# Copies of cached keys and values moved from the MLP to the projection, issued tile by tile

## The chip, the cores and the metric

The kernel runs on one core of one Trainium2 chip. The metric is the device time of one execution in microseconds, from the runs of the kernel on the chip; a profile of one execution gives the trace. SyncE (SP) only issues DMA transfers and waits on semaphores; ScalarE (ACT) computes and issues transfers too. TensorE is PE, VectorE is DVE, GpSimd is POOL.

## What is computed

One layer of a hybrid decoder for a prompt of 2048 rows and a sample group of 8 sequences with 8 rows each, all in float32. The part of the reference that the change touches is the new window of the sample group: the cached keys and values without their first 8 rows, and the 8 new rows behind them.

```python
D_MODEL, BATCH, SEQ, DEC_BATCH, DEC_SEQ = 1024, 1, 2048, 8, 8     # WB = 2048 cached rows, 8 heads of 64
def layer(hp, hs):
    a = mixer(rms_norm(h, norm1_g))        # proj = h @ w_in; dilated attention || mLSTM; @ w_out
    h = h + a
    h = h + square(relu(rms_norm(h, norm2_g) @ w_up)) @ w_down       # D_FF = 4096
# in the mixer of the sample group:
kc = concatenate([win_k, ka], axis=1)      # win_k: (8, 2048, 8, 64), ka: the 8 new rows
vc = concatenate([win_v, va], axis=1)
new_k, new_v = kc[:, -2048:], vc[:, -2048:]
```

Outputs are the final normalised rows, the new windows, and the mLSTM states.

## The kernel before

The program runs in stages: `project` (the input projection), `mixers` (attention and mLSTM), `project_out`, and `mlp`. Products are made in three parts of rounded numbers (high x high, low x high, high x low; `split_products`, L220 to L222), so each weight is rounded by ACT and its rest taken by POOL or DVE before PE can use it.

**The projection.** Rows are taken in two groups, of 8 and of 9 tiles of 128 rows. Per group PE makes 8 chunks of conv columns and then five token blocks b = 0 to 4 (`tokens`, q, k, v, output gate and mLSTM value), each of 512 columns for every tile of the group. A tile's products go to one of two banks in turn and add 1 to `tok_mm`; PE starts tile t+2 when DVE has emptied tile t (`tok_ready`). DVE empties a bank into a slot of `stage` (`tile_out`, L659 to L663); the first group uses two slots in turn, the second three, and DVE waits until the slot's last store has landed (`stage_out`). ACT issues that store (`keep`, L501) right after DVE. In the second group the last tile holds the sample's rows and is the eighth of nine in order; it needs two thirds of the products.

The weights of a block are loaded by SP into one buffer, `w_raw` (L368 in the first group, L372 in the second), as soon as the block before has been split from it (`lo_ready`). ACT rounds a block (`round_block`, L463) one block ahead of its use, between the stores of two blocks, and POOL takes the rests (L411). In the second group SP's queue also carries, in this order, the tables of the mLSTM gates: `sync_load` and `sync_ends` behind the load of block 2, `sync_m` (two round trips of the running maximum through DRAM), eight staged tiles (`load_tile`, L346) and `sync_weights` behind the load of block 3, then `sync_sample` and the other staged tiles behind the load of block 4. ACT reads the gate rows after the third tile of block 1 (`act_log`), DVE the maximum after the third tile of block 2.

```python
with sp.Fori(1, 5) as b:                                     # first group
    sp.wait_ge(lo_ready, b + (base + 8))
    sp.dma_start(w_raw[:], K.w_tok[b]).then_inc(wt_in, 16)
```

**The MLP.** Three groups of 6, 6 and 5 tiles; per group 16 steps f of 256 hidden columns. SP loads `wu_raw` (L2649) and `wd_raw` (L2652) when POOL is done with the buffer, and ahead of that each step issues two copies, `copy` (L2683): step f = 2i + j of group g copies the part 2g + j, of six, of the cached keys and of the values of sequence i. A copy is 340 rows of 2 KB, contiguous, from DRAM to DRAM; 3 groups x 16 steps x 2 make 96 copies. The steps 0 to 11 are a loop on SP, 12 to 15 are written out. The second and third group begin with loads of tiles of x (`load_x`, L2657) and of the residual (L2673). Nothing reads the copies; SP waits for all of them at the end of the program.

Of the kernel before, what the change touches and what calls it, by code (L numbers as in the profile page):

```python
# [16 lines left out]
DEC_B, DEC_T = 8, 8  # L17
# [10 lines left out]
WB = 2048  # L28
# [213 lines left out]
def project(K):  # L242

    nc, sem = K.nc, K.sem
# [5 lines left out]
    with ExitStack() as ctx:  # L251
# [77 lines left out]
        def _(sp):  # L329
# [11 lines left out]
            def load_tile(x):  # L341
# [3 lines left out]
                    rows = rows.rearrange("(e u) c -> u e c", u=16)  # L345
                sp.dma_start(staged[:, x], rows).then_inc(staged_in, 16)  # L346

            for g in range(2):
                if g == 0:
                    norm.sync_group(sp, GN[0], constants)  # L350
                else:
                    for T in range(GT0[1], GT0[1] + GN[1]):
                        norm.load(sp, T, T % 2, False)
                        if T == GT0[1] + 1:
                            sp.wait_ge(lo_ready, 13)
                            load_first()
                base = 13 * g
                sp.wait_ge(norm.xn_ready, 8 + 8 * g)
                sp.dma_start(wq_raw, K.w_qk[1]).then_inc(wq_in, 16)
                sp.wait_ge(qk_mm, QB[g] + NPC[g])  # L360
                sp.dma_start(w_raw[:], K.w_tok[0]).then_inc(wt_in, 16)
                with sp.Fori(2, 8) as c:
                    sp.wait_ge(lo_ready, c + base)
                    sp.dma_start(wq_raw, K.w_qk[c]).then_inc(wq_in, 16)
                if g == 0:
                    with sp.Fori(1, 5) as b:
                        sp.wait_ge(lo_ready, b + (base + 8))
                        sp.dma_start(w_raw[:], K.w_tok[b]).then_inc(wt_in, 16)  # L368
                    continue
                for b in range(1, 5):  # L370
                    sp.wait_ge(lo_ready, b + (base + 8))
                    sp.dma_start(w_raw[:], K.w_tok[b]).then_inc(wt_in, 16)  # L372
                    if b == 2:
                        for s in range(2):
                            sp.wait_ge(acc_out[s], 16 * 8)
                        sp.wait_ge(conv_out, 16)
                        tables.sync_load(sp)
                        tables.sync_ends(sp)
                    if b == 3:
                        tables.sync_m(sp)  # L380
                        for s in range(3):
                            sp.wait_ge(stage_out[s], 16 * (6 + (20 if s < 2 else 0)))
                        for x in range(24, 32):
                            load_tile(x)
                        tables.sync_weights(sp)
# [2206 lines left out]
def mlp(K):  # L2592
# [7 lines left out]
    FB = DFF // 256  # L2600
    G = len(GN)
    with ExitStack() as ctx:
# [20 lines left out]
        assert nc.sbuf_base <= K.front_at + 4 * TOP  # L2623
        bank = K.bank

        acc_in, y_out, copied = sem("mlp_acc_in"), sem("mlp_y_out"), sem("mlp_copied")
        wu_in, wu_hi_ready, wu_lo_ready = M.wu_in, M.wu_hi_ready, M.wu_lo_ready
        wd_in, wd_hi_ready, wd_lo_ready = sem("mlp_wd_in"), sem("mlp_wd_hi"), sem("mlp_wd_lo")
        up_mm, u2_ready, u_hi_ready, u_lo_ready = sem("mlp_up_mm"), sem("mlp_u2"), sem("mlp_u_hi"), sem("mlp_u_lo")
# [13 lines left out]
        block = ctx.enter_context(nc.Block(no_gpsimd_drain=True))  # L2643
        @block.sync
        def _(sp):
            CB = (WB - DEC_T) // 6

            def load_up(E, f):
                sp.dma_start(wu_raw[:], K.ins["w_up"][f]).then_inc(wu_in, 16)  # L2649

# [8 lines left out]
            for g in range(G):  # L2659
# [18 lines left out]
                    sp.wait_ge(wd_lo_ready, 1)  # L2678
                    load_down(1, 1)

                def copy(i, j):
                    for name in ("k", "v"):
                        sp.dma_start(K.o[f"win_{name}_sample"][0].rearrange("b s h d -> b s (h d)")[i, CB * (2 * g + j):CB * (2 * g + j + 1), :],  # L2683
                                     K.ins["cache_" + name][i, DEC_T + CB * (2 * g + j):DEC_T + CB * (2 * g + j + 1), :])\
                            .then_inc(copied, 16)

                def step(i, j, up=None, down=None):

                    f = 2 * i + j
                    copy(i, j)  # L2690
                    if up is not None:
                        sp.wait_ge(wu_lo_ready, f + (FB * g + 3))
                        load_up(0, up)
                    if down is not None:
                        sp.wait_ge(wd_lo_ready, f + (FB * g + 2))
                        load_down(0, down)
# [6 lines left out]
                        step(i, j, 2 * i + j + 3, 2 * i + j + 2)  # L2703
                for f in range(12, FB):
                    more = g < G - 1
                    step(f // 2, f % 2, (f + 3) % FB if more or f + 3 < FB else None,
                         (f + 2) % FB if f + 2 < FB or (more and f + 2 == FB) else None)
            for i, t in enumerate(ORDER[G - 1]):
# [4 lines left out]
                    sp.wait_ge(y_last, 1)  # L2713
                dst = K.o["y_prompt"][0, T * P:(T + 1) * P, :] if T < TILES - 1 else K.o["y_sample"].rearrange("b t d -> (b t) d")
                sp.dma_start(dst, acc[0:(P if T < TILES - 1 else NS), t]).then_inc(y_out, 16)
            sp.wait_ge(copied, 16 * 2 * G * FB)

        @block.gpsimd
        def _(pool):
# [472 lines left out]
def hybrid_step(nc, ins, outs, debug=None):  # L3192
# [9 lines left out]
    def dram(name, shape):  # L3202
        kind = "ExternalOutput" if debug and name in debug else "Internal"
        return nc.dram_tensor(name, shape, F32, kind=kind).ap()

    K.proj = dram("proj", (5, ROWS, AW))
    K.win = {KK: outs["win_k_prompt"].rearrange("a z s h d -> (a z s) (h d)"),
             VK: outs["win_v_prompt"].rearrange("a z s h d -> (a z s) (h d)")}
# [10 lines left out]
    with ExitStack() as ctx:  # L3219
# [27 lines left out]
        with nc.sbuf_tensor("front", [P, FRONT], F32):  # L3247
            K.place = lambda name, at, shape, dt=F32: nc.alloc_sbuf_tensor_at(name, shape, dt, offset=front_at + 4 * at)
            K.stage_out = [sem(f"p1_stage_out{s}") for s in range(3)]
            kept = len(stage_sems)  # L3250
            project(K)
            end_stage(kept)
            mixers(K)
# [63 lines left out]
```

## Time and profile before

| | us |
|---|---|
| median of three runs | 2979.95 |
| lowest and highest run | 2974.84, 2980.64 |
| span of the profiled execution, first to last instruction | 2977.5 |
| PE busy in it | 2862.7 (96%) |
| DVE, ACT, POOL busy | 1429.0, 926.1, 1001.3 |

### The profile page before, as it was taken

What the parts mean: (1) busy time and instruction counts of PE and PEld (TensorE: products, weight loads), DVE (VectorE), ACT (ScalarE), POOL (GpSimd) and SP (SyncE); (2) the same over time, 40 slices, a digit from 0 to 9 for tenths busy, and PEclk for the clock granted to TensorE, in tenths of its full rate; (3) what the DMA queues carried; (4) which work ended last, traced back from release to release, by engine and by line L of the source; (5) the groups of instructions that cost most, each with busy time, mean ns of one, the idle gap of its engine ahead of it and who ended that gap; (6) DMA issues with size and microseconds to landing.
All of it is one profiled execution on the core that took longest, in us unless ns stands there. A gap on an engine that the chain in (4) does not pass through costs nothing.

```text
span 2977.5 us, 47544 instructions
## 1 busy us (share of the span) xinstructions
PE 2862.7 (96%) x18291; PEld 2482.8 (83%) x18291; DVE 1429.0 (48%) x3364; ACT 926.1 (31%) x1740; POOL 1001.3 (34%) x589
## 2 busy tenths in 40 slices
PE   7999999999999978999999999999999999999998
PEld 5878788887778757678899999989999998899997
DVE  5522555334788855676343333344333333544444
ACT  4301322112677742431122222243222222422222
POOL 1212012211445530210154343444434344545443
PEclk8999999999999988999999999999999999999999
DMA  4322223335364558945452322235222323533332
GB/s 137 113 103 95 99 95 121 107 111 156 121 204 144 163 179 324 392 150 186 147 197 97 123 94 108 97 120 226 94 108 96 125 94 117 208 126 134 139 127 84
DMA packets 124714, 421.28 MB, mean 141 GB/s; under 512 B 18639, under 2 KB 44371, under 8 KB 104838
## 3 DMA queue, kind: packets, MB, share of 16 engines
q1 hardware_dynamic: 104124, 367.71, 34.9%
q10 hardware_dynamic: 19290, 47.37, 4.1%
q0 software_dynamic: 1152, 4.19, 0.4%
q8 instruction: 97, 1.59, 0.2%
q14 instruction: 51, 0.42, 0.0%
HBM read 350.70 MB, written 135.63 MB: 163 GB/s over the span
## 4 chain that ended last, share of the span: by engine, by line
PE 47%; DVE 1%; DMA 1%; ACT 1%; POOL 0%; issue 0%; ACTq 0%; DVEq 0%
PE bank L220 15%; PE bank L222 15%; PE bank L221 15%; PE bank L236 0%; PE bank L235 0%; DMA mlp_acc<-x 0%; POOL mlp_wu_lo L2724 0%; DVE mlp_acc L2954 0%; DVE mlp_acc L2989 0%; DMA mlp_xb<-x 0%; PE bank L3099 0%; DVE mlp_xn L2942 0%; POOL mlp_xb L2766 0%; ACT mlp_wu_hi L2782 0%; DMA out_y_prompt<-mlp_acc 0%
## 5 line engine op out<-in xcount | busy, mean ns | idle before, releaser
L2954 DVE TENSOR_TENSOR mlp_acc<-mlp_acc,bank 128x512 f32<-128x512 f32 x542 | 348.2, 684 | 364.0 <-PE bank L222 355.6
L220 PE MATMUL bank<-mlp_hT_hi,mlp_wu_hi 128*128 128x384 f32 (+1 forms) x1536 | 496.6, 323 | 3.1 <-PEq L3243 3.1
L222 PE MATMUL bank<-mlp_hT_hi,mlp_wu_lo 128*128 128x384 f32 (+1 forms) x1536 | 495.4, 323 | 0.0
L221 PE MATMUL bank<-mlp_hT_lo,mlp_wu_hi 128*128 128x384 f32 (+1 forms) x1536 | 495.1, 322 | 0.0
L2942 DVE TENSOR_TENSOR mlp_xn<-mlp_xn 128x384 f32<-128x384 f32 (+1 forms) x192 | 204.6, 1071 | 510.4 <-ACT mlp_xn L2800 491.2
L220 PE MATMUL bank<-mlp_wd_hi,mlp_u_hi 128*128 128x512 f32 x1024 | 399.9, 391 | 5.0 <-DVE mlp_acc L2954 4.9
L221 PE MATMUL bank<-mlp_wd_lo,mlp_u_hi 128*128 128x512 f32 x1024 | 398.9, 390 | 0.0
L222 PE MATMUL bank<-mlp_wd_hi,mlp_u_lo 128*128 128x512 f32 x1024 | 398.8, 389 | 0.0
L2728 POOL TENSOR_TENSOR mlp_wd_lo<-mlp_wd_raw,mlp_wd_hi 128x2048 fp32r<-128x2048 f32 x48 | 222.0, 4625 | 391.6 <-ACT mlp_wd_hi L2788 391.6
L2737 POOL TENSOR_TENSOR mlp_u_lo<-mlp_xn,mlp_u_hi 128x384 fp32r<-128x384 f32 (+1 forms) x192 | 177.8, 937 | 360.5 <-ACT mlp_u_hi L2809 360.5
L220 PEld LDWEIGHTS bank<-mlp_hT_hi,mlp_wu_hi 128*128 128x128 f32 x1536 | 288.8, 188 | 5.2 <-issue 3.5
L221 PEld LDWEIGHTS bank<-mlp_hT_lo,mlp_wu_hi 128*128 128x128 f32 x1536 | 288.8, 188 | 1.8
L222 PEld LDWEIGHTS bank<-mlp_hT_hi,mlp_wu_lo 128*128 128x128 f32 x1536 | 288.8, 188 | 0.0
L220 PE MATMUL p_bank<-p_w_hi,p_hT_hi 128*128 128x512 f32 x640 | 251.5, 393 | 1.6 <-DVE p_stage L663 1.6
L221 PE MATMUL p_bank<-p_w_lo,p_hT_hi 128*128 128x512 f32 x640 | 250.7, 392 | 0.0
L222 PE MATMUL p_bank<-p_w_hi,p_hT_lo 128*128 128x512 f32 x640 | 250.7, 392 | 0.0
L2724 POOL TENSOR_TENSOR mlp_wu_lo<-mlp_wu_raw,mlp_wu_hi 128x2048 fp32r<-128x2048 f32 x47 | 217.1, 4619 | 94.8 <-ACT mlp_wu_hi L2782 94.8
L2800 ACT ACTIVATE mlp_xn<-bank 128x384 f32<-128x384 f32 (+1 forms) x192 | 89.1, 465 | 507.5 <-PE bank L222 490.3
L2788 ACT ACTIVATE mlp_wd_hi<-mlp_wd_raw 128x2048 fp32r<-128x2048 f32 x48 | 92.1, 1918 | 490.7 <-PE bank L222 489.5
L220 PEld LDWEIGHTS bank<-mlp_wd_hi,mlp_u_hi 128*128 128x128 f32 x1024 | 192.2, 188 | 44.4 <-issue 5.7
L222 PEld LDWEIGHTS bank<-mlp_wd_hi,mlp_u_lo 128*128 128x128 f32 x1024 | 192.3, 188 | 40.4
L221 PEld LDWEIGHTS bank<-mlp_wd_lo,mlp_u_hi 128*128 128x128 f32 x1024 | 192.3, 188 | 37.9
(377 smaller groups left out, 4702.7 us busy)
## 6 DMA issues: line engine op xcount, KB each, us to landing
mlp_wu_raw<-in_w_up SPq DMA_DIRECT2D x48, 1024.0 KB, 4.8
mlp_wd_raw<-in_w_down SPq DMA_DIRECT2D x48, 1024.0 KB
out_win_k_sample<-in_cache_k SPq DMA_DIRECT2D x48, 680.0 KB, 6.3
out_win_v_sample<-in_cache_v SPq DMA_DIRECT2D x48, 680.0 KB, 7.2
p_w_raw<-in_w_tok SPq DMA_DIRECT2D x10, 2048.0 KB
sm_vin<-in_cache_v SPq DMA_DIRECT2D x8, 2048.0 KB, 13.4
proj<-p_stage ACTq DMA_DIRECT2D x53, 256.0 KB, 2.0
parts<-mx_part SPq DMA_DIRECT2D x48, 264.0 KB, 3.6
```

The source lines that it names most:

```text
L220: nc.tensor.matmul(out, ah, bh, start=(k == 0), stop=False)
L221: nc.tensor.matmul(out, ah, bl, start=False, stop=False)
L222: ins = nc.tensor.matmul(out, al, bh, start=False, stop=(k == n - 1))
L2724: g_.tensor_tensor(wu_lo[s][:], wu_raw[:], wu_hi[s][:].bitcast(F32), ALU.subtract).then_inc(wu_lo_ready, 1)
L2728: g_.tensor_tensor(wd_lo[s][:], wd_raw[:], wd_hi[s][:].bitcast(F32), ALU.subtract).then_inc(wd_lo_ready, 1)
L2737: ins = g_.tensor_tensor(u_lo[s][:, m, cols], u2[:, m, cols], u_hi[s][:, m, cols].bitcast(F32), ALU.subtract)
L2788: A(wd_hi[s][:], wd_raw[:], ACT.Copy).then_inc(wd_hi_ready, 1)
L2800: A(u2[:, m, w * q:w * q + w], bank[k][:, 0:w], ACT.Relu).then_inc(relu_done, 1)
L2942: v.tensor_tensor(u2[:, m, w * q:w * q + w], u2[:, m, w * q:w * q + w], u2[:, m, w * q:w * q + w], ALU.mult).then_inc(u2_ready, 1)
L2954: ins = v.tensor_tensor(acc[:, t, 512 * e:512 * e + 512], acc[:, t, 512 * e:512 * e + 512], bank[4 + 2 * (i % 2) + e][:], ALU.add)
```

## The change

The copies are issued by a new helper, `copy_cache`, with the same size and the same rows. Sequences 0 to 5 (72 of the 96 copies) are copied from the projection's token blocks: `copies(i, ev)` issues six pairs (k and v) for sequence i, pair e once `tok_mm` has reached ev + e. In each group the sequences 3g, 3g + 1 and 3g + 2 go with the blocks 0, 1 and 2, from the end of the third tile to that of the eighth. In the second group the pairs of block 1 stand behind `sync_m`. Sequences 6 and 7 stay in the MLP, two copies at each of the steps 12 to 15 of the three groups. The semaphore that counts the copies now lives from the projection on.

```diff
+            def copies(i, ev):
+
+                for e in range(6):
+                    sp.wait_ge(tok_mm, ev + e)
+                    for name in "kv":
+                        K.copy_cache(sp, name, i, e)
...
-                if g == 0:
-                    with sp.Fori(1, 5) as b:
-                        sp.wait_ge(lo_ready, b + (base + 8))
-                        sp.dma_start(w_raw[:], K.w_tok[b]).then_inc(wt_in, 16)
-                    continue
                 for b in range(1, 5):
                     sp.wait_ge(lo_ready, b + (base + 8))
                     sp.dma_start(w_raw[:], K.w_tok[b]).then_inc(wt_in, 16)
+                    if g == 0 or b != 3:
+                        if b > 1:
+                            copies(3 * g + b - 2, 40 * g + GN[g] * (b - 2) + 3)
+                    if g == 0:
+                        continue
                     if b == 2:
...
                     if b == 3:
                         tables.sync_m(sp)
+                        copies(3 * g + b - 2, 40 * g + GN[g] * (b - 2) + 3)
...
-                def copy(i, j):
-                    for name in ("k", "v"):
-                        sp.dma_start(K.o[f"win_{name}_sample"][0].rearrange("b s h d -> b s (h d)")[i, CB * (2 * g + j):CB * (2 * g + j + 1), :],
-                                     K.ins["cache_" + name][i, DEC_T + CB * (2 * g + j):DEC_T + CB * (2 * g + j + 1), :])\
-                            .then_inc(copied, 16)
-
                 def step(i, j, up=None, down=None):
 
                     f = 2 * i + j
-                    copy(i, j)
...
                 for f in range(12, FB):
                     more = g < G - 1
+                    for name in "kv":
+                        K.copy_cache(sp, name, 6 + (4 * g + f - 12) // 6, (4 * g + f - 12) % 6)
...
-            sp.wait_ge(copied, 16 * 2 * G * FB)
+            sp.wait_ge(K.cache_out, 16 * 2 * 6 * DEC_B)
...
+    rows = (WB - DEC_T) // 6
+
+    def copy_cache(eng, name, b, e):
+        eng.dma_start(outs[f"win_{name}_sample"][0].rearrange("b s h d -> b s (h d)")[b, rows * e:rows * (e + 1), :],
+                      ins["cache_" + name][b, DEC_T + rows * e:DEC_T + rows * (e + 1), :]).then_inc(K.cache_out, 16)
```

SP's queue in the second group of the projection, from the loads of the blocks 1 and 2 to the staged tiles, before:

```order
L372 DMA p1_w_raw_72<-in_w_tok 128x4096 [waits p1_w_lo] x2
L875 DMA p1_gt_ig_82<-gate_rows 64x128 [waits p1_conv_out,p1_acc_out1,p1_acc_out0]
...
L887 DMA p1_gt_ends_98<-gate_ends 4x32x1 [waits gt_ends_out]
L372 DMA p1_w_raw_72<-in_w_tok 128x4096 [waits p1_w_lo]
L894 DMA gate_mprev<-p1_gt_msc_99 4x16x1 [waits gt_own]
...
L897 DMA out_m_prompt<-p1_gt_msc_99 4x1
L346 DMA p1_staged_79<-proj 128x512 [waits p1_stage_out2,p1_stage_out1,p1_stage_out0]
```

The same place with the change (L3210 is the copy; of each run of twelve the first pair stands here):

```order
L374 DMA p1_w_raw_72<-in_w_tok 128x4096 [waits p1_w_lo] x2
L3210 DMA out_win_k_sample<-in_cache_k 16x10880 [waits p1_tok_mm]
L3210 DMA out_win_v_sample<-in_cache_v 16x10880
...
L883 DMA p1_gt_ig_82<-gate_rows 64x128 [waits p1_conv_out,p1_acc_out1,p1_acc_out0]
...
L374 DMA p1_w_raw_72<-in_w_tok 128x4096 [waits p1_w_lo]
...
L905 DMA out_m_prompt<-p1_gt_msc_99 4x1
L3210 DMA out_win_k_sample<-in_cache_k 16x10880 [waits p1_tok_mm]
L3210 DMA out_win_v_sample<-in_cache_v 16x10880
...
L346 DMA p1_staged_79<-proj 128x512 [waits p1_stage_out2,p1_stage_out1,p1_stage_out0]
```

Each run of six pairs stands between a load of weights and the next entries of the gate tables; the order of all that was there is kept. PE, DVE, ACT and POOL have the same instructions in the same order as before.

SP's queue in the MLP at the head of the loop over the steps 0 to 11, before (semaphores bear the names that their numbers had in an earlier stage):

```order
L2701 ISA
L2683 DMA out_win_k_sample<-in_cache_k 16x10880
L2683 DMA out_win_v_sample<-in_cache_v 16x10880
...
L2649 ISA [waits p1_gate_mm]
L2649 DMA mlp_wu_raw_5017<-in_w_up 128x2048
...
L2652 ISA [waits p1_tabs_mm]
L2652 DMA mlp_wd_raw<-in_w_down 128x2048
```

With the change, where the last two rows are the first pair behind the loop, for step 12:

```order
L2700 ISA
L2655 ISA [waits p1_gate_mm]
L2655 DMA mlp_wu_raw_5118<-in_w_up 128x2048
...
L2658 ISA [waits p1_staged_in]
L2658 DMA mlp_wd_raw<-in_w_down 128x2048
...
L3210 DMA out_win_k_sample<-in_cache_k 16x10880
L3210 DMA out_win_v_sample<-in_cache_v 16x10880
```

The loop has lost its copies; the loads and their waits stand as before.

## Rows read from the trace of the kernel before

**Rows 1.** The page of before: span, busy time, and the slices of DMA.

```profile
span 2977.5 us, 47544 instructions
...
PE 2862.7 (96%) x18291; PEld 2482.8 (83%) x18291; DVE 1429.0 (48%) x3364; ACT 926.1 (31%) x1740; POOL 1001.3 (34%) x589
...
DMA  4322223335364558945452322235222323533332
```

**Rows 2.** The page, chain that ended last, by line.

```profile
PE bank L220 15%; PE bank L222 15%; PE bank L221 15%; PE bank L236 0%; PE bank L235 0%; DMA mlp_acc<-x 0%; POOL mlp_wu_lo L2724 0%; DVE mlp_acc L2954 0%; DVE mlp_acc L2989 0%; DMA mlp_xb<-x 0%; PE bank L3099 0%; DVE mlp_xn L2942 0%; POOL mlp_xb L2766 0%; ACT mlp_wu_hi L2782 0%; DMA out_y_prompt<-mlp_acc 0%
```

**Rows 3.** Window, MLP's first group: length, busy PE, PEld, DVE, ACT, POOL, PEclk, DMA share, GB/s.

```profile
1520.00:1960.00 440.00, 440.00 (x2229) 401.65 (x2228) 155.02 (x215) 97.31 (x131) 173.67 (x79) 1.00 0.29 106
```

**Rows 4.** Waits of SP's queue: us in total, times, longest.

```profile
SPq L2649 <- POOL mlp_wu_lo L2724: 643.3, 46, 16.8
```

**Rows 5.** Windows in the token blocks of the projection, and at its end.

```profile
575.00:600.00 25.00, 25.00 (x112) 20.71 (x111) 8.13 (x30) 4.81 (x6) 9.18 (x2) 1.00 0.45 128
...
700.00:725.00 25.00, 21.37 (x100) 18.44 (x99) 9.69 (x27) 3.29 (x5) 1.27 (x6) 0.86 0.23 80
```

**Rows 6.** Timeline of DVE, second group: start, us, instruction [idle before <-releaser].

```profile
497.06 0.30 DVE L659 TENSOR_TENSOR p_bank<-p_bank,p_rot 128x128 f32<-128x128 f32 x1 [3.96 <-PE p_bank L222]
...
502.50 0.30 DVE L659 TENSOR_TENSOR p_bank<-p_bank,p_rot 128x128 f32<-128x128 f32 x1 [3.96 <-PE p_bank L222]
...
577.57 0.30 DVE L659 TENSOR_TENSOR p_bank<-p_bank,p_rot 128x128 f32<-128x128 f32 x1 [5.05 <-DMA out_win_k_prompt<-p_stage]
```

**Rows 7.** Timeline of ACT, same stretch.

```profile
541.13 1.28 ACT L555 ACT_TABLE_LOAD   x1 [13.01 <-DVE p_stage L663]
...
577.31 1.92 ACT L463 ACTIVATE p_w_hi<-p_w_raw 128x2048 fp32r<-128x2048 f32 x1 [33.89 <-DMA p_w_raw<-in_w_tok]
...
620.10 3.74 ACT L463 ACTIVATE p_w_hi<-p_w_raw 128x2048 fp32r<-128x2048 f32 x2 [24.24 <-DVE p_stage L663]
```

**Rows 8.** The page, DMA issues: KB each, median us to landing.

```profile
out_win_k_sample<-in_cache_k SPq DMA_DIRECT2D x48, 680.0 KB, 6.3
...
proj<-p_stage ACTq DMA_DIRECT2D x53, 256.0 KB, 2.0
```

**Rows 9.** The chain in order of time: start, us, what; MLP, second group's start.

```profile
1988.33 3.43 DMA mlp_xb<-x
```

**Rows 10.** Window in the MLP in which only copies move.

```profile
1573.00:1577.00 4.00, 4.00 (x25) 4.00 (x24) 0.56 (x1) 0.91 (x2) 0.86 (x1) 1.00 0.92 389
```

**Rows 11.** First group: SP timeline, stores of tile p_stage, ACT timeline.

```profile
153.26 37.59 SPq L368 DMA_DIRECT2D p_w_raw<-in_w_tok  x2
...
190.52 45.04 SPq L368 DMA_DIRECT2D p_w_raw<-in_w_tok  x2
...
L501 ACTq DMA_DIRECT2D proj<-p_stage x4: 326/330/333, 143.0 to 157.0; - x4
...
316.01 1.06 ACT L110 ACTIVATE p_xn<-p_xb 128x1024 f32<-128x1024 f32 x1
```

**Rows 12.** Timeline of SP's queue, second group: start, us, what it issued.

```profile
498.64 0.42 SPq L877 DMA_DIRECT2D p_gt_col<-in_state_m  x1
...
561.29 0.37 SPq L372 DMA_DIRECT2D p_w_raw<-in_w_tok  x1
...
578.11 0.47 SPq L896 DMA_DIRECT2D p_gt_col<-gate_mprev  x1
...
602.13 0.43 SPq L372 DMA_DIRECT2D p_w_raw<-in_w_tok  x1
```

**Rows 13.** Tile p_stage: a store, and landings in the windows 498:500, 604:606, 560:580.

```profile
L501 ACTq DMA_DIRECT2D proj<-p_stage x1: 361/361/361, 498.6 to 498.6; - x1
...
DMA to landing us min/median/max: 5.8/5.8/5.8
...
DMA to landing us min/median/max: 10.2/10.2/10.2
...
DMA to landing us min/median/max: 2.2/7.6/14.3
```

More of the change, by code:

```diff
@@ L2624, in mlp @@
         bank = K.bank
-        acc_in, y_out, copied = sem("mlp_acc_in"), sem("mlp_y_out"), sem("mlp_copied")
+        acc_in, y_out = sem("mlp_acc_in"), sem("mlp_y_out")
         wu_in, wu_hi_ready, wu_lo_ready = M.wu_in, M.wu_hi_ready, M.wu_lo_ready
@@ L2645, in _ @@
         def _(sp):
-            CB = (WB - DEC_T) // 6
             def load_up(E, f):
@@ L3204, in dram @@
         return nc.dram_tensor(name, shape, F32, kind=kind).ap()
+    rows = (WB - DEC_T) // 6
+    def copy_cache(eng, name, b, e):
+        eng.dma_start(outs[f"win_{name}_sample"][0].rearrange("b s h d -> b s (h d)")[b, rows * e:rows * (e + 1), :],
+                      ins["cache_" + name][b, DEC_T + rows * e:DEC_T + rows * (e + 1), :]).then_inc(K.cache_out, 16)
+    K.copy_cache = copy_cache
     K.proj = dram("proj", (5, ROWS, AW))
@@ L3249, in hybrid_step @@
             K.stage_out = [sem(f"p1_stage_out{s}") for s in range(3)]
+            K.cache_out = sem("cache_out")
             kept = len(stage_sems)
```

## Prediction

> **What bounds the kernel now.** I read the page first. TensorE is busy in 96% of the span, and the slices show 9 in nearly all of them; the DMA slices stand mostly at 2 to 5, with 8 and 9 only in two slices in the middle [rows 1]. The chain that ended last is PE work at its three product lines, 15% each, and its DMA pieces round to 0% [rows 2]. So a copy from DRAM to DRAM costs time only where it makes PE wait, and I looked for that in the two places that the change touches.
>
> The place it leaves, the MLP: over the loop of the first group PE is busy 440.00 of 440.00 us at clock 1.00, with the DMA engines 0.29 busy at 106 GB/s [rows 3]. The DMA queue of SP is not late there either: it stood 643.3 us in 46 waits for POOL to be done with the up weights, so each load is issued as soon as its buffer is free [rows 4].
>
> The place it goes to, the token blocks of the projection: PE is busy 25.00 of 25.00 us in nearly every window there, as in [rows 5]. Every 5.44 us a tile's products end, DVE empties the bank (starts 497.06 and 502.50) and, 1.48 us later, waits 3.96 us for PE [rows 6]; ACT issues the store at 498.6, 1.54 us after DVE's start [rows 13]. Two margins follow. PE goes on with tile t+2 when DVE is done with t, so DVE may be 3.96 us late before PE is. A stage slot is used again after three tiles in the second group: 3 x 5.44 - 1.54 = 14.8 us for a store to land before DVE is late, and 18.7 us before PE is. With the two slots of the first group these are 9.3 and 13.3 us.
>
> **What the change removes.** 72 of the 96 copies leave the MLP (48 for k, as many for v, 680 KB each [rows 8]). A step of the loop is 33.1 us with two copies (1.39 MB): 42 of the 106 GB/s. What hid them was PE, busy without a gap, so I put their removal at 0. The other end, a gain: only the starts of the MLP's two later groups have DMA pieces on the chain, as the 3.43 us for a tile of x [rows 9] and one of the residual's loads. The copies of the last steps of each group stay where they are, ahead of those loads in the queue as before, and the first copies of a group are issued behind the residual's load in both kernels. So nothing there is freed; if half of the x pieces went anyway at both starts, that would be 3.4 us.
>
> **What it adds, first group.** 36 copies in pairs, at the ends of the tiles 3 to 8 of blocks 0 to 2. A stretch with only copies in it moved 389 GB/s [rows 10]: a pair of 1.39 MB takes 3.6 us, less than the tile's 5.44 us. A store lands 2.0 us after its issue when nothing is beside it [rows 8]; behind a lone pair it would take 5.6 us, below the 9.3. In blocks 1 and 2 the weight load (2.1 MB, 5.4 us at that rate) is issued early in the block (190.52, and 45.0 us later) and is over before the second pair: cost 0. Block 0 is tighter. Its load goes at 153.26. The four stores from 143.0 to 157.0 put the fourth tile's end at 155.5 and the third's at 150.1, so the first pair follows the load at once, the second at 155.5, the next two at 160.9 and 166.4: the queue is full from 154 to 174 us. The store issued at 157.0 [rows 11] lands after 5.6 us at best and, if it waits for all of that, at 175 us, 18 us after its issue, 4.7 us more than the 13.3 that PE leaves it. The tiles of x for the second group, issued right behind the load at 235.6 now, wait until block 2 is done (20 tiles after 155.5, about 267) and are first read at 316.01 [rows 11]: cost 0.
>
> **What it adds, second group.** Here pacing holds only in block 0.
> - Block 0: the weight load, issued just ahead of the gate rows, and twelve copies are 5.4 + 21.5 = 26.9 us of transfers, and the last pair goes at the end of the eighth tile, about 517 us (two tiles after 502.50 and the sample's, which takes two thirds). The queue is full without a pause until 523 us. The gate rows, issued up to 498.64 now [rows 12], come behind them, at some 518 to 521, and land near 525; ACT takes them up at 541.13 [rows 7]: 15 us of cover, cost 0.
> - Block 1's copies stand behind the running maximum, whose round trip ends at 578.11 [rows 12]. Their six waits ask for tiles that are done by about 565 us, so all twelve go at once from 579.4: 12 x 0.6 us of issue and 21.5 us of transfer, until about 601. Behind them are eight staged tiles, the gate rows, the broadcast and the load of block 4's weights (602.13 now [rows 12]). I expect that load at about 610. ACT rounds it at 620.10 [rows 7]; the slowest such load in the trace took 16.0 us (561.29 [rows 12] to 577.31 [rows 7]), so ACT may be 6 us late. PE needs those weights only after block 3, nine tiles after that (about 668): cost 0.
> - Block 2's copies follow that load: another twelve, of which ten have their tile done. The queue is full until about 637; the small gate tables behind them end near 650, before the staged loads that wait for block 3 in both kernels.
>
> What is left is ACT's stores, which go through the same 16 engines on their own queue, while SP's is full. The trace of before has this beside the 2.1 MB load alone: 5.8, 10.2 and once 14.3 us instead of 2.0 [rows 13]. The 14.3 made DVE wait 5.05 us [rows 6], and PE still had 25.00 of 25.00 us in that window [rows 5]. For a store beside twelve copies the bounds are 5.8 us and the whole burst, 21.5 + 2.0 = 23.5 us. I take 15 us at all these places, near the nearest row (14.3). With three slots that is just over the 14.8: DVE is late by a microsecond or so some four times, PE is not. The upper bound would pass the 18.7 by 4.8 us at two places, 9.6 us in all; I allow a tenth of that, 1 us. In block 0 of the first group 15 us pass the 13.3 by 1.7 us; since the earlier pairs are soon through I take 1 us there.
>
> The Trainium skill, "DMA: Bandwidth & Descriptors", section on queues, rings and completion order, says that each DMA engine takes turns between its queues, one packet each. By that rule the 8 packets that a store has on an engine each stand behind one copy's packet of 1.8 us, 14.4 + 2.0 = 16.4 us. That is under the 18.7 of the second group, where the sum would then be 0 in place of the 9.6 of a whole burst, and 3.1 us over the 13.3 of the first. No row of before shows it beside packets as large as a copy's.
>
> **Sum.** The span was 2977.5 us [rows 1]; the median of the three runs, 2979.95, lies 2.45 us above it. 2977.5 + 0 (MLP) + 1 (first group) + 1 (second group) + 2.45 = 2982 us. A difference of 0.2%, 6 us, is about what a measurement of this kernel can tell from none.
>
> **Rivals.**
> - *The stores become the bound (slower).* The stores land more than 13.3 us (first group) or 18.7 us (second) after their issue, DVE waits on the stage slot and PE on DVE. For it: four stretches of 20 us and more without a pause in SP's queue, where one load of 5.4 us already made 14.3. Against it: the second group's third slot. Price if stores wait for the whole stretch: 4.7 in the first group; 2 x 4.8 at the bursts; in block 0 of the second group a store issued at 504.0 waits for 523 + 2, 21 - 18.7 = 2.3: 16.6 us. Where PE stood at the end of the stage the window's clock fell to 0.86 [rows 5], half speed for 7 us or 3.5 us of work, which could come on top once. The case decides from an excess of 6 us on; its middle, half of 16.6 + 3.5, gives 2990 us, its end 3000.
> - *The MLP gives time back (faster).* Weights and x land sooner when the queue is emptier. For it: the DMA pieces of the chain [rows 9]. Against: a PE without gaps, and copies that stay at those very places. Both x pieces gone are 6.9 us: 2973.
> - *It does not do what it says.* Pacing fails in blocks 1 and 2 of the second group, as above; that is in my forecast and in the first rival, by its effect on the stores.
>
> **How the numbers follow.** Hidden but for a few microseconds: 0.58, by itself 2974 to 2986. Stores bind: 0.34. MLP faster: 0.08. These are the chances of same, slower and faster. The range takes all of the forecast's case and the slower one up to three quarters of its price (16.6 x 0.75 + 2 = 14.5): 2974 to 2994.
>
> **What would show it.** Right: in the MLP loop PE's busy share and the product durations unchanged, DMA share down from 0.29 to below 0.2; copies in SP's queue in pairs at each tile's end in the first group, in bursts from about 579 and 610 us; store landings of 10 to 16 us there; DVE idle "DMA <- p_stage" of a few us and PE within a microsecond of 25.00 per window; the projection's end moved by less than 3 us. Wrong: PE below 24 us in a window between 500 and 660 us or a clock under 1.00 there, stores landing after 18.7 us, or an MLP whose length changes. PE late between 160 and 185 us by over 3 us would mean that I took the first group's stores too short.

## Result and profile after

The changed kernel is slower: 3004.14 us median of 4 runs (3003.27 to 3006.69) against 2977.39 us for the kernel before on the same chip (4 runs, 2974.12 to 2980.64). The ratio is 1.0089, 95% interval 1.0075 to 1.0104: 26.7 us or 0.9% more. The prediction said 2982 us, range 2974 to 2994. The time lies outside the range. It is the first rival, the stores that become the bound, and more than the price that I gave it (2990 us, at its end 3000). All ratios compare undisturbed runs; one run each of `held`, of `held2` and of the kernel before beside it stood far above the others and is left out of them.

The page of the changed kernel, span, TensorE and the DMA slices, which answer to [rows 1]. The profiled execution took 3003.59 us.

```profile
span 3001.8 us, 47341 instructions
...
PE 2869.2 (96%) x18291; PEld 2486.1 (83%) x18291; DVE 1429.2 (48%) x3364; ACT 925.7 (31%) x1740; POOL 1001.3 (33%) x589
...
DMA  3386225485455448955342121234111222422222
```

DMA work has moved from the slices of the MLP to those of the projection, and the span is 24.3 us longer. To find where, I set the start of each of the 18,291 products against that of the same product before. The difference is 0 until 150 us; 6.9 after block 0 of the first group; 12.3 after block 0 of the second; 14.7 after block 1; 25.8 after block 2 and until the projection's end. The mixers give 1.5 back. In the MLP it then stays at 24.2 to 24.4 from the first product to the last. Everything was lost in four places of the projection, and nothing was won in the MLP.

Windows of the changed kernel: length, busy time of PE, PEld, DVE, ACT, POOL, granted clock, DMA share, GB/s. The last answers to [rows 3], the others to [rows 5].

```profile
150.00:175.00 25.00, 23.05 (x103) 18.74 (x102) 5.77 (x20) 0.00 (x0) 3.00 (x1) 1.00 0.92 333
175.00:200.00 25.00, 22.04 (x89) 17.55 (x88) 5.77 (x20) 3.72 (x2) 9.17 (x2) 0.93 0.58 200
525.00:550.00 25.00, 21.44 (x87) 16.96 (x86) 7.16 (x22) 3.73 (x2) 9.18 (x2) 0.93 0.51 180
600.00:625.00 25.00, 22.89 (x102) 18.62 (x101) 7.62 (x29) 1.08 (x4) 0.00 (x0) 1.00 0.99 329
650.00:675.00 25.00, 15.65 (x61) 12.23 (x60) 3.19 (x12) 3.24 (x5) 6.86 (x2) 0.80 0.84 281
1544.00:1984.00 440.00, 440.00 (x2229) 401.58 (x2228) 154.86 (x215) 97.07 (x130) 173.99 (x79) 1.00 0.21 74
```

In the MLP the DMA share fell from 0.29 to 0.21 and PE has no gap, as before. In the projection PE stands still in the five windows shown, for 9.35 us in the fifth. Waits in the window 100:745 (us in total, times, longest):

```profile
DVE p_bank L667 <- DMA proj<-p_stage: 46.2, 7, 16.7
...
DVE p_bank L667 <- DMA out_win_v_prompt<-p_stage: 29.6, 5, 7.8
...
PE p_bank L220 <- DVE p_stage L671: 19.5, 5, 9.4
```

DVE waits for stage slots whose stores have not landed, and PE for DVE. PE's row is the waits of 1.96, 2.96, 3.56 and 9.35 us and one of 1.65 us at 230 us that the kernel before has as well; the fifth new one, of 2.11 us at 623 us, ends at another line. The new waits come to 19.9 us. How long the stores take shows in the tile `p_stage` of the changed kernel, in the windows 155:175, 505:523 and 651:654 (us from issue to landing):

```profile
DMA to landing us min/median/max: 9.1/14.9/18.0
...
DMA to landing us min/median/max: 14.8/16.9/19.7
...
DMA to landing us min/median/max: 17.1/21.8/22.1
```

The last window is the costly one. SP's queue in it, which answers to the last line of [rows 12] (start, us, instruction):

```profile
591.03 0.57 SPq L3210 DMA_DIRECT2D out_win_k_sample<-in_cache_k  x1
...
603.69 11.53 SPq L346 DMA_DIRECT2D p_staged<-out_win_k_prompt  x1
615.27 3.41 SPq L912 DMA_DIRECT2D ng_rows<-p_gt_ng  x1
618.72 0.59 SPq L914 DMA_DIRECT2D gate_wti<-p_gt_col  x1
635.99 0.33 SPq L917 DMA_DIRECT2D wti<-gate_wti  x1
636.36 0.43 SPq L374 DMA_DIRECT2D p_w_raw<-in_w_tok  x1
```

A burst of twelve copies starts at 591.03. The last staged tile then takes 11.53 us to be issued, the gate table is issued at 618.72, and its landing, which the next instruction waits for, takes until 635.99. So block 4's weight load goes out at 636.36, against 602.13 before and my 610. Some 12 of these 34 us are what the earlier places had lost by then; against the products the load is about 22 us late. ACT meets it, as in [rows 7], here with what follows:

```profile
637.01 0.36 ACTq L509 DMA_DIRECT2D out_win_v_prompt<-p_stage  x1
645.68 3.73 ACT L471 ACTIVATE p_w_hi<-p_w_raw 128x2048 fp32r<-128x2048 f32 x2 [37.56 <-DMA p_w_raw<-in_w_tok]
...
651.38 0.33 ACTq L509 DMA_DIRECT2D proj<-p_stage  x1
...
652.43 0.33 ACTq L509 DMA_DIRECT2D proj<-p_stage  x1
...
653.47 0.33 ACTq L509 DMA_DIRECT2D proj<-p_stage  x1
```

ACT works in order. It waits for the load before it issues the next stores, so three go out within 2.1 us, beside the third burst of copies, and they are the ones that land after 17.1 to 22.1 us. The first of them lands at 668.5, which ends DVE's wait and then PE's, in their timelines:

```profile
668.62 0.30 DVE L667 TENSOR_TENSOR p_bank<-p_bank,p_rot 128x128 f32<-128x128 f32 x1 [16.71 <-DMA proj<-p_stage]
```

```profile
670.15 0.80 PE L220 MATMUL p_bank<-p_w_hi,p_hT_hi 128*128 128x512 f32 x1 [9.35 <-DVE p_stage L671]
```

### The profile page after: what moved, and what is told of

The parts are those of the page before. It is cut to its first block, busy times and chain, and to the rows that moved or that the text cites. A ratio compares the mean times of both kernels' runs of the same rounds, so it can differ in the third digit from the quotient of the medians.

```text
span 3001.8 us, 47341 instructions
## 1 busy us (share of the span) xinstructions
PE 2869.2 (96%) x18291; PEld 2486.1 (83%) x18291; DVE 1429.2 (48%) x3364; ACT 925.7 (31%) x1740; POOL 1001.3 (33%) x589
## 2 busy tenths in 40 slices
DMA packets 124714, 421.28 MB, mean 140 GB/s; under 512 B 18639, under 2 KB 44371, under 8 KB 104838
## 4 chain that ended last, share of the span: by engine, by line
PE 47%; DVE 1%; DMA 1%; ACT 1%; POOL 0%; issue 0%; ACTq 0%; DVEq 0%
PE bank L220 15%; PE bank L222 15%; PE bank L221 15%; PE bank L235 0%; PE bank L236 0%; DMA mlp_acc<-x 0%; POOL mlp_wu_lo L2725 0%; DVE mlp_acc L2955 0%; DVE mlp_acc L2990 0%; DMA mlp_xb<-x 0%; PE bank L3100 0%; DVE mlp_xn L2943 0%; POOL mlp_xb L2767 0%; ACT mlp_wu_hi L2783 0%; DMA out_y_prompt<-mlp_acc 0%
```

## Experiments

All are timed against the kernel before, whose median was 2977.3 to 2977.9 us beside these runs. The ratios are the ones on record; the ratio of two medians comes out about 0.1% apart from them at most (1.0050 for `half`, 1.0074 for `gentle`). A gap below is time in which PE stands, as its timeline gives it; what the clock costs behind a gap comes on top. Four theories stood when they began. A: each DMA engine takes turns between SP's queue and ACT's, so the copies' large packets (43.5 KB, sixteen to a copy) hold up the stores. B: what counts is bytes in flight. C: the largest piece comes from block 4's held weight load. D: the MLP hides the copies wholly, so nothing could be won.

| kernel | median us | ratio to before, 95% |
|---|---|---|
| changed kernel | 3004.14 | 1.0089 (1.0075 to 1.0104) |
| small | 3002.16 | 1.0085 (1.0072 to 1.0098) |
| half | 2992.58 | 1.0041 (1.0025 to 1.0057) |
| tiny | 2981.68 | 1.0008 (0.9996 to 1.0021) |
| g0_only | 2987.04 | 1.0027 (1.0017 to 1.0037) |
| g1_only | 2995.82 | 1.0056 (1.0043 to 1.0069) |
| no_copies | 2980.03 | 1.0000 (0.9989 to 1.0011) |
| late | 2995.62 | 1.0063 (1.0050 to 1.0076) |
| tiny_late | 2978.24 | 1.0002 (0.9992 to 1.0012) |
| held | 2977.36 | 1.0000 (0.9991 to 1.0009) |
| held2 | 2979.57 | 1.0004 (0.9990 to 1.0017) |
| gentle | 2999.77 | 1.0063 (1.0047 to 1.0078) |
| gentle2 | 2982.11 | 1.0019 (1.0008 to 1.0030) |
| gentle2_tiny | 2979.67 | 1.0003 (0.9993 to 1.0014) |

### The size of a copy's packets

First try (`small`), in the helper that issues a copy:

```diff
+        cut = lambda a: a.rearrange("s c -> (s c)").rearrange("(p f) -> p f", p=128)
```

> The changed kernel with each copy cut into 128 pieces of 5.4 KB instead of 16 of 43.5 KB, the same bytes, the same places in SyncE's queue. Theory A (each DMA engine takes a packet of one queue and then one of the other, so a 43.5 KB packet of 1.6 us stands ahead of every 2 KB packet of a store of ScalarE's queue): the turn falls to 0.2 us, a store of 8 packets per engine beside copies lands in 3 to 5 us instead of 15 to 20, the waits of VectorE and TensorE on p_stage go, and about 15 to 23 of the 26.7 us come back (2981 to 2989 us). Theory B (what counts is the bytes that are in flight, not the piece they come in): landings and the time stay as they were, 3004 us, within 3 us.

1.0085 and landings of 15.7 to 20.9 us in the window 505:523: as the changed kernel. By its own wording that was theory B. But the page's packet counts were those of the changed kernel to the last one:

```profile
DMA packets 124714, 421.28 MB, mean 141 GB/s; under 512 B 18639, under 2 KB 44371, under 8 KB 104838
```

The 128 pieces follow each other in memory on both sides, and were joined again into 16 packets. The run tried nothing; it is a second measurement of the changed kernel. The next two put the pieces in an order in which neighbours are not adjacent:

```diff
+        cut = lambda t: t.rearrange("s c -> (s c)").rearrange("(a b f) -> b a f", a=8, b=16)
```

with `a=8` in `tiny` and `a=2` in `half` (32 pieces of 21.8 KB); `cut` is put around the source and the destination.

> The changed kernel with each copy's 16 pieces of 43.5 KB cut into 128 of 5.4 KB, this time in an order in which no two neighbours follow each other in memory, so that they can't be joined (the first try left the packet counts as they were, so it tried nothing). Packets under 8 KB should rise by 96 x 128 = 12288. Theory A (each DMA engine takes turns between the two queues packet by packet, 8 packets of a store at 1.6 to 1.9 us each are 13 to 15 us): stores issued beside the weight load and copies land in 3 to 7 us instead of 15 to 20, the gaps of TensorE shrink to those of the held weight load at most, 10 to 23 us come back. Theory B (bytes in flight or memory bandwidth): landings stay at 15 to 20 us and the time within 4 us of 3002 to 3004 us.

> The changed kernel with each copy in 32 pieces of 21.8 KB that can't be joined. Theory A: a store of 8 packets per engine lands in about half the time beside copies (8 to 11 us against 15 to 20), and the time lies between the changed kernel's and that with 5.4 KB pieces. Theory B: no difference to the changed kernel.

The page of `tiny` has 12,288 more packets under 8 KB, the 96 x 128 that were meant:

```profile
DMA packets 135466, 421.28 MB, mean 141 GB/s; under 512 B 18639, under 2 KB 44371, under 8 KB 117126
```

The bytes and SP's order are the same, and the ratio falls from 1.0089 to 1.0041 and 1.0008. The landings in the window 505:523, of `half` and then of `tiny`, against 14.8/16.9/19.7:

```profile
DMA to landing us min/median/max: 11.5/13.9/15.2
```

```profile
DMA to landing us min/median/max: 8.2/8.4/8.7
```

B falls. A holds in its direction: the larger the pieces, the later the stores land. It does not hold in its count, one packet each in turn, as the last section shows, and for `tiny` I had expected 3 to 7 us. The order of the pieces changed together with their size; no run changed the order alone, and what speaks for the size is that `half` lies between the two. Block 0's windows of `tiny`, with 307 and 320 GB/s in them (PE alone; clock, DMA share, GB/s):

```profile
150.00:175.00 25.00, 25.00 (x112) 1.00 0.87 307
175.00:200.00 25.00, 25.00 (x109) 1.00 0.89 320
```

A DMA system that is 0.87 to 0.89 busy does not slow TensorE. What is left in `tiny` is one gap of 3.9 us at 649 us, taken up below; with the half clock behind it the place lost 6.6 us. The stores of `half` landed near the margins (13.3 and 18.7 us in the prediction), and its gaps are 7.4 us at 653 us, 1.4 us near 180 and, beyond the 1.65 us of the kernel before, 1.3 us at 223.

### The two groups apart

One group's copies stay in the projection (three of the six parts of six sequences), the others go out in every second step of the MLP loop.

```diff
-                    if g == 0 or b != 3:
+                    if g == 0:
...
+                        if j == 0:
+                            for name in "kv":
+                                K.copy_cache(sp, name, i, 3 + g)
```

> Copies in the first group of the projection alone (3 of 6 parts of six sequences); the others are issued in the MLP, one pair in every second of its steps. If the losses are local and add up, this one has the first group's 6.2 us of gaps and 1.5 to 2 us of half clock: 7 to 9 us over the kernel before (2984 to 2987 us). If the loss lies in the second group alone, or is a cost of the copies wherever they stand, it is at the time before (within 2 us), or at 3004 us.

> Copies in the second group of the projection alone; the others in the MLP. If the losses are local and add up: 16.9 us of gaps and some 6 us of half clock less what the mixers give back, 17 to 20 us over the kernel before (2994 to 2998 us). The sum of this run's excess and that of the first group alone should be the 26.7 us of the whole change, within 3 us.

0.27% and 0.56%, that is 8.0 and 16.7 us of 2977; together 24.7 against 26.7 for the whole change (by the medians 9.2 and 17.9, together 27.1). The losses are local and add up. In `g0_only` PE has no gap in the stretches of the second group where the change lost time, in `g1_only` none in the first group's (windows of each, PE alone; clock, DMA share, GB/s):

```profile
520.00:560.00 40.00, 40.00 (x175) 1.00 0.14 53
600.00:670.00 70.00, 70.00 (x305) 1.00 0.34 110
```

```profile
150.00:200.00 50.00, 50.00 (x219) 1.00 0.36 132
```

### Was there anything to win

`no_copies` is the kernel before without its 96 cache copies; the windows of the sampled sequences stay without their cached rows.

```diff
-                    copy(i, j)
...
-            sp.wait_ge(copied, 16 * 2 * G * FB)
```

> The kernel before without its 96 cache copies anywhere (the output windows of keys and values of the sampled sequences are left without their cached rows). Theory D (the MLP is bound by TensorE at full clock and hides the copies wholly, so that no place for them could bring anything): 2977 to 2978 us as the kernel before, within 3 us. If the copies cost something in the MLP, through its transfers or its clock, it is 5 us or more faster, and there was something to win.

Ratio 1.0000 (0.9989 to 1.0011). From the MLP's first product to its last it took 1489.8 us, as before and as the changed kernel (1489.8 and 1489.7). D holds, within 3 us: where taking the copies away gains nothing, no placing of them has anything to gain.

### The held weight load

`late` puts the second group's later copies behind block 4's load and paces them by the blocks 2 and 3:

```diff
...
+                    if g == 1 and b == 4:
+                        copies(4, 61)
+                        copies(5, 70)
...
-                        copies(3 * g + b - 2, 40 * g + GN[g] * (b - 2) + 3)
```

> The changed kernel with the second group's copies of block 1 put behind block 4's weight load and paced by block 2's tiles, and the last ones paced by block 3's tiles. Theory C (the largest loss, 10.3 us without products at 660 to 670 us and 5 us of half clock behind it, comes from block 4's weight load, which is held at SyncE behind a burst of 12 copies, tables and their slow landings until 636 us): the load goes out at about 602 us as before the change, ScalarE's round of it waits no more, no three stores are issued together, and 12 to 16 us come back (2988 to 2992 us). Rival: the stores are slow beside any copies, wherever the load is: the pairs that are now paced cost 1 us per tile or more, and less than 5 us come back (above 2999 us).

`tiny_late` is the same with 5.4 KB pieces:

> The changed kernel with 5.4 KB pieces, and the second group's later copies behind block 4's weight load. The 5.4 KB pieces alone left one gap of TensorE, 4.9 us at 649 us with 7 us of half clock behind it, after block 4's weight load at 628 us. Theory C (that gap is the held load: ScalarE rounds late and sends three stores together): the load goes out by 613 us, the gap goes and 4 to 7 us of profiled span come back, median 2976 to 2981 us. If not C but the stores' landing times make that gap, it stays and so does the time.

`late`: the load went out at 612.16 (not 602: the gate tables ahead of it were themselves 10 us late, and the products 9), the gap of 9.35 us at 660 us is gone, and 0.26% or 7.7 us came back by the ratios (8.5 us by the medians), less than the 12 to 16 expected. Copies still start right behind the load, five pairs of them at once (612.6 to 619.1), since their tiles were done; the stores of 612 to 630 landed after 13.1 to 21.6 us, and two gaps of 1.6 and 2.2 us stand at 638 and 646 us. `tiny_late`: the load went out at 603.54, no gap, 1.0002. The gap of `tiny` goes with the held load. Both runs move the burst ahead of the load together with it, so the load has to be tried alone.

Is a late load enough by itself? `held` is the kernel before, copies in the MLP, and its load held to the point of block 2 where the change sends it:

```diff
+                    if b == 4:
+                        sp.wait_ge(tok_mm, 40 + 27)
```

> The kernel before, its copies in the MLP as they were, with block 4's weight load held at SyncE until block 2's last tile is multiplied (the point at which the change sent it out): about 617 to 620 us instead of 602. Theory C in its strong form (the late load alone stops TensorE, since ScalarE's stores wait behind its round): a gap of 4 to 10 us in block 3, and 5 to 12 us over the kernel before with the clock. In its weak form (the late load needs slow stores beside it, which land in 16 to 22 us; here they land in 2 to 4): a gap under 2 us, and 0 to 3 us over the kernel before.

It went out at 617.16. ACT was as late against its block as in the changed kernel: 14.1 us between the last store of block 2 (618.67) and the next (632.74), there 14.4 (637.01 to 651.38). Timeline of ACT in `held`:

```profile
618.67 0.34 ACTq L503 DMA_DIRECT2D out_win_v_prompt<-p_stage  x1
627.03 3.73 ACT L465 ACTIVATE p_w_hi<-p_w_raw 128x2048 fp32r<-128x2048 f32 x2 [32.17 <-DMA p_w_raw<-in_w_tok]
...
632.74 0.33 ACTq L503 DMA_DIRECT2D proj<-p_stage  x1
```

No gap, and 1.0000. `held2` holds it two tiles longer (`40 + 29`):

> As the last run, with block 4's weight load held two tiles longer, to about 628 us, where the kernel with 5.4 KB pieces had it and stopped TensorE for 4.9 us. If a load held that long is enough by itself (three stores together at 642 to 644 us, ScalarE too late for the stage buffers' turn), a gap of 2 to 6 us in block 3 and 2 to 8 us over the kernel before. If it takes slow stores as well (they land in 2 to 4 us here), no gap over 1 us and the time of the kernel before within 2 us.

It went out at 626.76; four stores were issued together from 640.2 to 644.5 and landed after 2.0 to 2.5 us. One gap of 0.3 us (window of `held2`, same columns), 1.0004 (0.9990 to 1.0017):

```profile
625.00:650.00 25.00, 24.66 (x106) 1.00 0.42 139
```

Theory C falls in its strong form. Against the products the load was 27 us late in `held2`, more than the 22 us of the change and the 23 us of `tiny`. Such a load costs next to nothing where stores land in 2 us; beside stores of 8 to 12 us the gap was 3.9 us (`tiny`), and beside 17 to 22 us it was 9.35 (the change). It takes both to fill the three slots.

### A gentler placing

No copies right behind a weight load: the first group starts two tiles later, the second group's go behind the gate tables and by later tiles.

```diff
-                    if g == 0 or b != 3:
-                        if b > 1:
-                            copies(3 * g + b - 2, 40 * g + GN[g] * (b - 2) + 3)
+                    if g == 0 and b > 1:
+                        copies(b - 2, 8 * (b - 2) + 5)
+                    if g == 1 and b == 4:
+                        copies(4, 64)
+                        copies(5, 70)
...
                         tables.sync_load(sp)
                         tables.sync_ends(sp)
+                        copies(3, 45)
...
-                        copies(3 * g + b - 2, 40 * g + GN[g] * (b - 2) + 3)
```

> The changed kernel with its copies as they are in size, but no burst and none right behind a 2 MB weight load: in the first group they start 2 tiles later, in the second behind the gates' tables, paced by block 0's tiles from the 5th, by block 2's from the 5th and by block 3's. Lone pairs landed beside stores of 7 to 8 us without a wait of TensorE in the runs so far. If it is the pile of weight load and copies that delays the stores, the gaps at 170 to 182, 529, 621 to 671 us all go, and the time is 2976 to 2982 us. If lone pairs cost by themselves (bandwidth, clock), it stays above 2988 us.

The first group is whole, with the full-size packets (windows of `gentle`, same columns):

```profile
150.00:175.00 25.00, 25.00 (x112) 1.00 0.83 280
175.00:200.00 25.00, 25.00 (x109) 1.00 0.88 306
```

Its stores in the window 155:175 land in 4.9 to 7.6 us. The second group is not: `sync_ends` waits until 561 us, and the twelve copies meant for block 0 went in one burst right ahead of block 3's load (571.12). ACT waited 55.2 us in one piece for that load, and PE stood for 11.5 us between 582 and 613 us, and for another 4.6 us between 646 and 657. I had read the waits in front of my copies, not their times. `gentle2` puts `copies(3, 45)` between the two table calls, and `gentle2_tiny` adds the 5.4 KB pieces:

> As the last gentle run, with the second group's first 12 copies put between the gates' loads and the wait for their ends, so that they are paced by block 0's tiles from the 5th (the last run had them behind that wait, at 561 us, in a burst right ahead of block 3's weight load). The first group ran without a gap that way. If lone pairs away from the weight loads cost nothing, no gap is left in either group and the time is that of the kernel before: 2976 to 2981 us. If the second group's loads are held all the same (two pairs behind a table's or a load's wait), 4 to 12 us over the kernel before.

> The same placing with each copy in 128 pieces of 5.4 KB. It can at best be the kernel before, since that without any copies was not faster: 2976 to 2980 us by both theories; below 2973 us would show something that neither has. If pieces matter (A) it is not slower than the placing with 43.5 KB pieces.

`gentle2`: 1.0019 (1.0008 to 1.0030), two gaps of 0.5 and 1.1 us at 627 and 633 us. There the tile that the first pair waits for was done when the load went out (601.37), and the pair followed it at 601.85, so the stores from 603 to 618 landed after 13.2 to 19.4 us. `gentle2_tiny`: no gap in the projection, 1.0003. It is equal to the kernel before, and by D nothing better was to be had; no version beats it.

## Why the prediction was wrong

Point by point:

- **MLP, 0 us.** Right in time. DMA share 0.21, where I said below 0.2; length unchanged to 0.1 us; and `no_copies` shows that even all 96 copies were free there.
- **The chain from copies to stores to DVE to PE.** Right as a mechanism, and the four stretches that I listed are the four that lost time. The case had 0.34 and the wrong size. What the chain lacked is ACT, which a late load holds back from its stores.
- **"For a store beside twelve copies ... I take 15 us at all these places."** This is one of the two steps that failed; with what follows from it, it stands for three of the four places, 14.7 of the 25.8 us. In the second group's block 0 the four stores landed after 14.8 to 19.7 us (mean of the middle two 16.9), in the bursts up to 20.7 and 22.1. I chose by the nearest row, the 14.3 of [rows 13], which was measured beside packets of 16 KB. The stores that ended with a wait of PE's took 14.9 and 18.0 us in the first group, 18.8, 20.7 and 17.1 in the second: in the upper half between the ends of 5.8 and 23.5. What PE feels is the latest of them, and I priced all with one middle value.
- **"DVE is late by a microsecond or so some four times, PE is not."** It follows from the 15, and from margins that treat a store as if it came alone. DVE waited 14 times for the landing of a store in the projection, 88 us in all (7 waits of 46.2 us for `proj`, as shown, 5 of 29.6 for `out_win_v_prompt`, 2 others of 12.4). In block 0 of the second group the sample's tile is the eighth of nine, with products two thirds as long, and it takes the 18.7 us down by 1.8. The store issued at 510.9 landed after 18.8, DVE waited 7.86 us for it and PE 3.56 (timeline of DVE in the changed kernel):

```profile
520.47 0.30 DVE L667 TENSOR_TENSOR p_bank<-p_bank,p_rot 128x128 f32<-128x128 f32 x1 [4.16 <-DMA proj<-p_stage]
529.81 0.69 DVE L664 COPY p_xn<-p_bank 64x512 f32<-64x512 f32 x1 [7.86 <-DMA proj<-p_stage]
```

- **First group, 1 us.** It lost 6.9, of which PE stood for 4.9. The upper bound stood in the text, 18 us for one store and 4.7 us; 18.0 was measured, for the store at 162.4, behind one of 14.9 at 156.9. Two late stores in a row on two slots cost 1.96 and 2.96 us (PE's waits), with a short stretch at half clock.
- **Second group, blocks 1 and 2: load at "about 610", cost 0.** This is the other step that failed, and the costlier one: a term put at 0 that measured 11.1 of the 25.8 us. I counted 0.6 us for each issue of the staged tiles and the tables, and none of their landings: it went at 636.36. I had 48 us until PE needs those weights, which is true and was not the deadline; the deadline is ACT's next store. `held2` shows that this term needs slow stores to cost, `late` and `tiny_late` that the largest loss goes when it goes. A better size for the stores would not have found it: the store that ended PE's wait took 17.1 us, and with my 15 us in its place DVE would still have been late enough for a gap of some 7 us (an estimate: 9.35 less 2.1). In block 1's burst, where the load itself does no harm yet, 2.4 us were lost to the stores alone.
- **The clock on top of the rival, 3.5 us.** Too small in all, though less than thought in the largest place: there the clock fell in the gap and the half-speed stretch lay mostly inside it. Windows 665:670 and 670:675, the latter with 4.85 us busy at 0.65:

```profile
665.00:670.00 5.00, 0.00 (x0) 0.00 (x0) 1.35 (x5) 0.00 (x0) 0.00 (x0) 0.50 0.86 300
670.00:675.00 5.00, 4.85 (x14) 3.88 (x15) 0.40 (x3) 0.63 (x1) 0.00 (x0) 0.65 0.36 109
```

By these shares and the 0.82 of the window before them, half speed was granted for 10.2 us from about 663, and 7 of these us lie in the gap, which ends at 670.15. The place lost 11.1 us, of which PE stood for 9.35; the remaining 1.8 are the half speed behind the gap. The other three places lost 14.7 us in all, of which PE stood for 10.6. So 5.9 of the 25.8 us are no standing time, where I had 3.5 once.
- **The rule of the Trainium skill** ("DMA: Bandwidth & Descriptors", queues, rings and completion order), turns between queues packet by packet, gave an estimate of 16.4 us, against 14.8 to 22.1 measured. `half` and `tiny` agree with it in that smaller packets land the stores sooner. The count that I made from it does not hold: the section's packet is a group of descriptors, and I set one 2 KB row of the profile against one row of a copy. In the trace two store rows leave for one copy row, 8 us of turns and not 14.4, and some 7 us of other waits ahead and behind bring the sum near my number, as the last section tells. That it came close is luck. Used as the choice instead of the 14.3, it would have priced the first group at 3.1 and still left the second at 0.

## What to carry over

Before a transfer is moved under a stage with spare bandwidth, ask how large its packets are and which small transfer on another queue has a deadline there: cut the pieces (in an order that can't be joined) and keep them away from the large loads, one pair per tile. Price a queue by the landings that it waits for and by what the engine behind a load does next in its program, not by when the loaded data is needed. And first take the work out altogether: if that gains nothing, no placing will.

## What the runs showed of the hardware

- A copy from DRAM to DRAM of 680 KB that is contiguous is 16 packets of 43.5 KB, each 1.9 us long beside stores. Cutting it into 128 adjacent pieces leaves the packets as they were (124,714 in all, with and without the cut); in a permuted order it becomes 128 packets of 5.4 KB and 0.21 us.
- In the packet records of the changed kernel, for the store issued at 156.9 us, the first of its 128 packets of 2 KB (84 ns each) leaves 3.5 us after the issue. Then about 32 leave in every 2 us, beside some 16 of 43.5 KB, and the 128 take 7.9 us; the landing comes 3.5 us after the last: 14.9 us. In `half` the 128 take 5.9 us and in `tiny` 2.8 us, the start is again 3.5 us after the issue, and the landings are at 10.8 and 7.5 us. Beside the 5.4 KB packets it is nearly one to one: 105 of the store against 110 in the first 2 us. So the piece size acts on the stretch in which the packets leave and on what follows it. Why 3.5 us pass ahead of the first packet at all three sizes, and what the last 3.5 us are, was not tried apart and stays open.
- A lone pair of copies per tile, away from a load, made stores land in 5 to 8 us and cost nothing measurable (`gentle`, first group, at 280 to 306 GB/s).
- Packets of 5.4 KB cost little bandwidth: in the same window, 505:530, `tiny` moved 354 GB/s and the changed kernel 381; the most that `tiny` showed in 25 us was 371 (632.5:657.5). The window 630:655 of `tiny`, with the held load's gap in it (PE alone; clock, DMA share, GB/s):

```profile
630.00:655.00 25.00, 21.12 (x88) 0.94 0.97 353
```
